# Four small changes of order around the boundaries between the twelve sub-layers of a denoising trunk

## What is computed

```python
def rmsnorm(x, g):
    y = x * lax.rsqrt(jnp.mean(x * x, axis=-1, keepdims=True) + EPS)
    return y * g

def modulate(x, shift, scale):
    return x * (1 + scale) + shift

def ffn_sublayer(x, shift, scale, gate, g_pre, g_post, w_in, w_out):
    h = modulate(rmsnorm(x, g_pre), shift, scale)
    a, b = jnp.split(h @ w_in, 2, axis=-1)
    h = (jax.nn.silu(a) * b) @ w_out
    return x + FFN_RES * gate * rmsnorm(h, g_post)
```

## Time and profile before

| what | value |
|---|---|
| median of 3 runs | 3085.76 us (3085.74 to 3086.63) |
| the profiled execution's own time | 3085.63 us |
| its span, first to last instruction | 3083.6 us |
| mean granted TensorE clock | 0.993 of full |
| PE busy | 2989.8 us, 97% |
| DVE busy | 2186.3 us, 71% |
| ACT busy | 1134.1 us, 37% |
| POOL busy | 585.4 us, 19% |
| HBM traffic | 166 GB/s over the span |

### The profile page before, as it was taken

The page is one execution under the profiler, slowest core; times in us unless marked ns, Lnnn a source line. Parts: engine busy times, 40 slices in busy tenths (PEclk is TensorE's granted clock), DMA queues, the critical chain, the costliest instruction groups (busy, mean ns, idle before and its releaser), DMA issues. The chain is left out here.

```text
span 3083.6 us, 48618 instructions
## 1 busy us (share of the span) xinstructions
PE 2989.8 (97%) x19442; PEld 2773.7 (90%) x19442; DVE 2186.3 (71%) x2829; ACT 1134.1 (37%) x1925; POOL 585.4 (19%) x586
## 2 busy tenths in 40 slices
PE   6999989999999999999999999989999999989999
PEld 6999878999999898999899999979998999978998
DVE  5887577887887656788877575658887888575444
ACT  4222564223422424222422354343224222564222
POOL 1112112112211102112211143531122112111001
PEclk9999999999999999999999999999999999999999
DMA  8667406666665445766566443227665666314443
GB/s 292 205 208 221 150 25 191 207 213 188 198 205 173 115 135 166 221 207 197 176 214 187 121 122 97 91 87 232 209 207 180 209 205 205 116 28 134 130 124 95
DMA packets 565509, 515.72 MB, mean 167 GB/s; under 512 B 42965, under 2 KB 499238, under 8 KB 563494
## 3 DMA queue, kind: packets, MB, share of 16 engines
q1 hardware_dynamic: 564726, 512.37, 54.2%
q10 hardware_dynamic: 560, 0.25, 0.0%
HBM read 509.31 MB, written 3.24 MB: 166 GB/s over the span
## 5 line engine op out<-in xcount | busy, mean ns | idle before, releaser
L1534 PE MATMUL bank<-h_hi,w_hi 128*128 128x384 f32 x3328 | 1119.3, 336 | 0.5 <-ACT tmp L1813 0.5
L1536 PE MATMUL bank<-h_hi,w_lo 128*128 128x384 f32 x3328 | 1114.7, 335 | 0.0
L1535 PE MATMUL bank<-h_lo,w_hi 128*128 128x384 f32 x3328 | 1113.4, 335 | 0.3 <-issue 0.3
L1794 ACT ACTIVATE w_hi<-raw 128x1024 fp32r<-128x1024 f32 x648 | 681.8, 1061 | 1026.7 <-PE bank L1536 485.9
L1952 DVE TENSOR_TENSOR w_lo<-raw,w_hi 128x1024 fp32r<-128x1024 f32 x648 | 807.6, 1270 | 349.8 <-ACT w_hi L1794 345.2
L1974 DVE SCALAR_TENSOR_TENSOR fold<-ada_raw,cond,fold 128x1024 f32<-128x1024 f32 x462 | 638.5, 1438 | 0.0
L1534 PEld LDWEIGHTS bank<-h_hi,w_hi 128*128 128x128 f32 x3328 | 625.3, 188 | 8.6 <-issue 0.8
L1535 PEld LDWEIGHTS bank<-h_lo,w_hi 128*128 128x128 f32 x3328 | 625.3, 188 | 6.2
L1536 PEld LDWEIGHTS bank<-h_hi,w_lo 128*128 128x128 f32 x3328 | 625.0, 188 | 0.4 <-issue 0.4
L2271 POOL TENSOR_TENSOR h_lo<-tmp,h_hi 128x384 fp32r<-128x384 f32 x176 | 281.5, 1599 | 1751.9 <-DVE h_hi L2008 1751.9
L1579 PE MATMUL bank<-w_hi,h_hi 128*128 128x512 f32 x1056 | 415.6, 394 | 5.6 <-DVE mod L1988 4.9
(11 more groups left out here) (201 smaller groups left out, 2403.6 us busy)
## 6 DMA issues: line engine op xcount, KB each, us to landing
raw<-w_ffn_in SPq DMA_DIRECT2D x352, 512.0 KB, 5.0
ada_raw<-w_ada SPq DMA_DIRECT2D x272, 512.0 KB, 4.2
raw<-w_ffn_out SPq DMA_DIRECT2D x176, 512.0 KB, 4.7
raw<-w_hgrn_in SPq DMA_DIRECT2D x40, 512.0 KB, 4.0
g_rows<-g_dram SPq DMA_DIRECT2D x12, 1024.0 KB, 7.0
raw<-w_attn_qkv SPq DMA_DIRECT2D x24, 512.0 KB, 5.6
raw<-w_conv_in SPq DMA_DIRECT2D x24, 512.0 KB, 4.9
ada_first<-w_ada SPq DMA_DIRECT2D x16, 512.0 KB, 12.4
```

What stands on the lines that cost most here:

```text
L1534: mm(out, wh, h_hi[:, k, :], start=(k == 0), stop=False)
L1535: mm(out, wh, h_lo[:, k, :], start=False, stop=False)
L1536: last = mm(out, wl, h_hi[:, k, :], start=False, stop=(k == DC - 1))
L1794: A(w_hi[:, b % RING, :], raw[:, b % RAW, :], ACT.Copy).then_inc(w_hi_made, 1)
```

## The change

- In out_tail, tile 0 is computed in another order: the first three chunks for half 0, then for half 1, then the fourth chunk for half 0 and for half 1 (before: all four chunks of half 0, then all four of half 1). PE waits for a chunk's h2_lo when it comes to it in half 0.
- The wait for mods_made at f = 21, where a unit is folded there, stands behind out_tail's products and the transposes of tile 1, as a wait for the units of the whole sub-layer.
- first_blocks makes the low products by halves of the k-rows, half 1 first for both blocks, then half 0, and waits for the low parts of each half by itself. Both blocks' ends (block_done) come in the second round.
- DVE's hi_of(e, 1, 1) goes ahead of hi_last(e, 0).
- POOL starts lo_half when hi_of(e, 1, 1) is done (before: when the last hn is made), and does half 1 of tiles 0 and 1 first, then half 0.
- ACT runs a one-column Silu at the start of a boundary behind attention or scan, and a one-column Exp at the start of attention, so that the tables are loaded there.
- The last stores go by column halves, six transfers instead of three.

```diff
         def store(dst, t):
-            sp.wait_ge(y_made, 2 * NT * (N_SUB - 1) + 2 * t + 2)
-            sp.dma_start(dst, y[:, t, :]).then_inc(out_stored, 16)
+            for n in range(2):
+                sp.wait_ge(y_made, 2 * NT * (N_SUB - 1) + 2 * t + n + 1)
+                sp.dma_start(dst[:, columns(n)], y[:, t, columns(n)]).then_inc(out_stored, 16)
...
-            pe.wait_ge(h_lo_made, 2 * (NT - 1) * (s + 1))
-            pe.wait_ge(h_lo_last, 2 * (s + 1))
-            for j, bank in enumerate(banks):
-                for k in range(DC):
-                    last = mm(psum[bank][:, 0:T], w_hi[:, (b0 + j) % RING, k * P:(k + 1) * P], h_lo[:, k, :],
-                              start=False, stop=(k == DC - 1), skip_group_check=True)
-                last.then_inc(block_done, 1)
+            for half in (1, 0):
+                pe.wait_ge(h_lo_made, (NT - 1) * (2 * (s + 1) - half))
+                pe.wait_ge(h_lo_last, 2 * (s + 1) - half)
+                for j, bank in enumerate(banks):
+                    for k in range(4 * half, 4 * half + 4):
+                        last = mm(psum[bank][:, 0:T], w_hi[:, (b0 + j) % RING, k * P:(k + 1) * P], h_lo[:, k, :],
+                                  start=False, stop=(k == 3), skip_group_check=True)
+                    if half == 0:
+                        last.then_inc(block_done, 1)
...
         def out_tail(s, chunks, b):
             e = s + 1
+            order = [(n, i) for n in range(2) for i in range(TAIL)]
+            late_last = [(n, i) for n in range(2) for i in range(TAIL - 1)] + [(0, TAIL - 1), (1, TAIL - 1)]
             for t in range(NT):
-                for n in range(2):
-                    for i, c in enumerate(chunks):
...
+                for n, i in late_last if t == 0 else order:
...
                 turn_normed(e, 1)
                 if sub_kind[s] == "ffn":
                     pe.wait_ge(a_read, FC * (ffn_number(s) + 1))
                     pe.wait_ge(b_read, FC * (ffn_number(s) + 1))
+                    need(pe, mods_made, units_end[s])
...
-                if f in folds:
+                if f in folds and f < FC - 1:
                     pe.wait_ge(mods_made, folds[f] + 1)
...
+            if sub_kind[s] == "attn":
+                load_table(ACT.Exp)
...
+        def load_table(function):
+
+            A(small[:, 28:29], ones[:, 0:1], function)
+
         def boundary(e):
+            if e > 0 and sub_kind[e - 1] in ("attn", "hgrn"):
+                load_table(ACT.Silu)
...
                 normed(e, 2)
+                hi_of(e, 1, 1)
                 hi_last(e, 0)
-                hi_of(e, 1, 1)
                 hi_last(e, 1)
...
-                gp.wait_ge(hn_made, 2 * NT * (e + 1))
-                for t in range(NT - 1):
-                    lo_half(e, t, 0)
-                    lo_half(e, t, 1)
+                gp.wait_ge(h_high_made, 2 * (NT * e + NT - 2) + 2)
+                for half in (1, 0):
+                    for t in range(NT - 1):
+                        lo_half(e, t, half)
```

More of the change, by code:

```diff
@@ L1519, in _ @@
             store(outs["y_sample"][0, (t - 1) * P:t * P, :], t)
-        sp.wait_ge(out_stored, 16 * (NT + stores_until(N_SUB)))
+        sp.wait_ge(out_stored, 16 * (2 * NT + stores_until(N_SUB)))
     @blk.tensor
@@ L1618, in out_tail @@
             e = s + 1
+            order = [(n, i) for n in range(2) for i in range(TAIL)]
+            late_last = [(n, i) for n in range(2) for i in range(TAIL - 1)] + [(0, TAIL - 1), (1, TAIL - 1)]
             for t in range(NT):
-                for n in range(2):
-                    for i, c in enumerate(chunks):
[L1622 to L1631, removed]
+                for n, i in late_last if t == 0 else order:
+                    if t == 0 and n == 0:
+                        pe.wait_ge(w_lo_made, b + i + 1)
+                        out_ready(s, chunks[i])
+                    hi, lo = moving_out(s, chunks[i])
+                    last = out_half(b + i, t, n, hi, lo, False, i == TAIL - 1)
+                    if t == NT - 1 and n == 1:
+                        last.then_inc(block_done, 1)
+                    elif i == TAIL - 1:
                         last.then_inc(acc_done, 1)
+                    if t == NT - 1 and n == 0 and i == 0 and e < N_SUB:
+                        turn_normed(e, 0)
             if e < N_SUB:
```

## The result

The changed kernel takes 3068.66 us (median of 4 runs, 3066.74 to 3070.67) against 3086.2 us: ratio 0.9937, 95% interval 0.9922 to 0.9952. Forecast were 3067.2 us, 18.5 us less than before; the medians are 17.5 us apart, and the profiled executions 18.9 us (3066.74 against 3085.63; spans 3064.8 and 3083.6). The four runs of the changed kernel lie in two pairs, 3066.74 and 3066.87, 3070.45 and 3070.67; the profile shows one of the faster pair.

The account below looks back on a forecast made before the run. PE was taken as the bound, so only its waits or slow stretches could be shortened. The terms 6.3 + 10.7 + 0.8 + 0.1 + 0.6 = 18.5 us gave 3067.2 us from a median of 3085.76, range 3061.5 to 3076.

Parts of the forecast that it names:

- Steps 1 and 2: PE's tail: modulation and last h2 low-part waits go, 6.3 us; tile 0's half 0 ending later costs 0.
- step 2: Tile 0's half 0 ends 9 products later; taken as 0, at most 0.7 us per boundary if squares or og queue.
- chain rival: Tile 0's later half 0 delays its chain at eleven boundaries: 7.7 us less gain, 3074.9 us; chance 0.04.
- step 4: Low products by row halves at boundaries; block A ends later, so Silu about 0.1 us late into an FFN.
- Steps 3 and 4: DVE/POOL reorder and halved low products: 1.3 us per boundary into an FFN, 1.4 into a mixer, 10.7 us together.
- port rival: DVE gets between POOL's operations only once all are through: 8.5 us less gain, 3075.7 us; chance 0.10.
- Step 5: Three of eleven boundaries stay at half clock, gaining about 0.1 us or nothing, since slow products are laid bare.
- Step 6: Function tables loaded at the boundary's start: 0.8 us into sub-layer 2 with clock and restart; Exp load nothing.
- Step 7: Last stores by halves, the first leaving about 0.7 us earlier: 0.6 us gained, between 0 and 0.7.
- slower rival: PE-bound half-clock stretches multiply; two at each of eleven boundaries cost 37 us, some 3104 us; chance 0.04.

Follow-up runs that it names:

- tail_only: Kernel before with only tile 0's new order and the modulation wait moved behind the tail: 3081.0 us, ratio 0.9974.
- warm_before: Kernel before plus eight useless 128-column products ahead of the last tile's transposes: 3087.76 us, ratio 0.9994.
- order_only: Kernel before with only the new DVE and POOL order and low products by halves; tail, tables and stores as before: 3078.87 us, ratio 0.9967.
- turn_later: Changed kernel with tile 0's transposes one chunk later in the last tile's products: 3064.57 us.
- no_halves: Changed kernel with the low products undivided, as before; new DVE and POOL order kept: 3078.12 us in one run.
- dve_old_order: Changed kernel with hi_of(1,1) behind hi_last(0) on DVE again, POOL still starting behind hi_of(1,1): 3083.63 us in one run.

## Why the prediction was right, step by step

The forecast was right in size and in nearly all its working. That it came within 0.4 us of the profiled executions' difference, and 1 us of the medians', is in part luck: the touched stretches gave 20.7 us instead of 18.5, since one boundary was at half clock and not three, and 2 us went the other way in stretches that the forecast left out. The terms, against the table above:

- **Steps 1 and 2, tail: 6.3 forecast, 6.9 measured alone** (tail_only), with hn's wait unchanged, so 0 for step 2 was right and the chain rival is refuted. In the changed kernel the same stretches give 5.9 (4.8 + 0.75, and 0.35 of sub-layer 11's 1.0): they begin at the next block, and carry Silu's wait of step 4, 0.13 us in each of eight FFNs (263.67 us against tail_only's 263.53). The 0.1 us for the restart came out at the five waits of 0.99 us (1.08 gained). At the three of 0.2 us the gain was 0.5, so there 0.3 us went beyond the wait itself; why is open.
- **Steps 3 and 4, 1.3 and 1.4 us per boundary at full clock: measured 1.2 into an FFN, 1.36 to 1.40 into a mixer.** Up to the next block it is 1.32 to 1.34 into an FFN; the 0.13 us of Silu's wait come behind that mark. The sum allowed 0.1 us for it at five FFNs, and it stands at all eight. The high products took 4.09 us instead of the 4.0 put for "no stop": the first two operations of hi_last(1) end 3.50 us behind the transposes, just ahead of the second half of the products at 3.56. The reading of how DVE and POOL hold each other up (DVE's SBUF-to-SBUF operation waits for the POOL operation under way, then gets in) holds to 0.1 us: lo_last(1) was put 4.15 us behind the transposes and starts at 4.25, the pair's end was put at 6.85 and is 6.79. The port rival is refuted by it, since DVE's first low part is through at 5.08 and POOL's fourth operation at 6.24. The Silu was to be about 0.1 us late; it holds PE's weight loads for 0.2 us at eight FFNs, 0.13 of it in the products:

```profile
PEld bank L1535 <- ACT tmp L1818: 1.6, 8, 0.2
```

- **Step 5, half clock: the mechanism was right, the count was not.** I kept three boundaries of eleven; the profile has one, into 6, where the gain is 0.04 us. Two more at full clock are worth 2.6 us, and that is by how much the boundaries gave more up to the next block (14.2 instead of 11.6; less Silu's 1.0, 13.2). The asymmetry that I argued from stands in the stretches: in the kernel before, the boundaries into 5 and 10 take 9.78 us at half clock and the others 9.77 to 9.82 at full; in the changed kernel the one at half clock takes 9.73 and the others 8.42 to 8.45. warm_before agrees: with no boundary at half clock the kernel before gains nothing.
- **Step 6, tables: 0.8 into 2, measured 2.0 with the clock's part** (that boundary was at half clock before and is not now). "Once of three; with step 4 at all three" is shown by order_only's three waits of 1.1. The drain of about 1.38 us that the Trainium skill (ScalarE: Activation LUTs, What ACT_TABLE_LOAD costs) adds is not in this trace, where the moved load is followed at once by the activation:

```profile
468.20 1.28 ACT L1891 ACT_TABLE_LOAD   x1
469.49 0.20 ACT L1891 ACTIVATE small<-ones 128x1 f32<-128x1 f32 x1
470.57 0.60 ACT L1862 ACTIVATE tmp<-bank 128x512 f32<-128x512 f32 x1 [0.88 <-PE bank L1584]
```

ACT then waits 0.88 us for PE; into 11 it waits 0.24 us. So the load is early enough at both. The one-column activation takes the 0.2 us assumed.
- **Step 7, stores: 0.6 forecast, 0.6 measured** (from DVE's last end to the end of the span 2.4 us instead of 3.05). Each half lands 2.0 us after issue instead of 2.6:

```profile
y_sample<-y SPq DMA_DIRECT2D x4, 256.0 KB, 2.0
```

- **What I left out: 2 us went the other way**, 1.4 of them in the scan. The scan is not touched, and in the fourteen profiles of this case its stretch runs from 273.1 us (warm_before) to 278.6 (order_only), with idle time of PE that the profile puts down to nothing (5.0 to 9.1 us) and 6.8 to 13.7 us at half clock. The two shortest (273.1 and 274.1) have 6.8 us at half clock, the three longest (278.0 to 278.6) 13.7. The profiles before and after both have 10.2, and 1.0 of the 1.4 us is in idle time put down to nothing (5.5 and 6.5 us). Both kernels lie within the spread; whether the change moved the scan at all is open.

The prediction's slower rival, half clock multiplying, did show a piece of itself: turn_later has seven boundaries at half clock. Even there they cost 0.9 to 1.3 us each, no more than what the edits had given.

## What to carry to other kernels

A wait at a boundary is worth what the next-late thing leaves of it, so put a number on that thing before summing. Here the low products could come no earlier than PE's own high products allowed, 5.57 us behind the transposes, and ACT's modulation left only 0.5 of the 1.2 us that DVE's new order seemed to free. Two engines whose operations hold each other up interact by the order in which single operations begin. So fix the start of the one that nobody waits for by a signal, at a place where it can't meet the critical one, and take two operations due within 0.02 us of each other as a risk. In this kernel half clock at a boundary cost nothing while DVE's chain was later than PE; once that chain is shortened it costs 0.9 to 1.3 us. Filling the gap in front of the transposes kept the clock up in four profiles of four; it pays only if the filler's length is read from a trace first.

## What the runs showed of the hardware

- A gap of about 1 us on PE (0.93 to 1.02) can be followed by a stretch at half clock. Over ten profiles without useless products 18 of 110 boundaries were hit, from none (no_halves, dve_old_order) to seven of eleven (turn_later); over the four with them none of 44, with the gap for the last transposes at 0 to 0.07 us. Why turn_later has seven and its neighbours at most three is not settled; its gap was 1.0 us instead of 0.93.
- A plain float32 product of 128 columns is issued as two instructions of 0.11 us (16 for eight), while a float32 transpose of the same size is one (8 for eight).
- Of two operations of DVE and POOL due within 0.02 us of each other, now the one and now the other went first (DVE at three boundaries, POOL at eight of one execution). As the loser DVE took 1.85 us instead of 0.69, POOL 1.83 instead of 1.3.
